# A two-block transformer kernel on one core: the end of the last down-projection and the final norm

## What is computed

```python
T, D, D_FF = 256, 2048, 8192
u = rms_norm_2(h, norm_mlp[l]) @ w_up[l]              # [T, 8192]
h = h + jnp.square(jax.nn.relu(u)) @ w_down[l]        # [T, 2048]
return rms_norm_2(h, norm_final)                      # h * rsqrt(mean(h*h) + 1e-5) * norm_final
```

## Time and profile before

| what | value |
|---|---|
| median of 3 runs | 2543.62 us (2541.82 to 2546.07) |
| span of the profiled execution, first to last instruction | 2541.9 us |
| the profiled execution's own time | the page gives none beside the span |
| PE busy | 2398.7 us (94%) |
| DVE busy | 1389.0 us (55%) |
| ACT busy | 1095.0 us (43%) |
| POOL busy | 48.4 us (2%) |
| chain that ended last: PE banks L2349 | 56% of the span |
| HBM read, written | 491.77 MB, 3.67 MB |

### The profile page before, as it was taken

One profiled execution on the slowest core, in us unless ns is written; L12 is line 12 of the kernel. 1 busy time (PEld: TensorE's weight loads), 2 busy tenths in 40 slices (PEclk: granted clock), 3 DMA queues, 4 the chain that ended last, 5 costly groups with the idle time before them and its releaser, 6 DMA issues.

```text
span 2541.9 us, 29777 instructions
## 1 busy us (share of the span) xinstructions
PE 2398.7 (94%) x12196; PEld 1917.1 (75%) x12196; DVE 1389.0 (55%) x1295; ACT 1095.0 (43%) x1099; POOL 48.4 (2%) x77
## 2 busy tenths in 40 slices
PE   5899999999999999999999679999999999999996
PEld 0487778887577788877887567788888888888885
DVE  0344335556846786666456774655555445545443
ACT  0455545333344444545354533456544434334332
POOL 0100000001000000000000000000000000000000
PEclk6899999999999999999999889999999999999998
DMA  9965455558976696555555001654555555565562
GB/s 391 385 197 156 142 166 168 178 184 319 421 252 201 230 370 198 207 166 172 182 183 166 11 18 31 240 175 161 170 182 183 190 192 190 189 193 188 183 198 99
DMA packets 223184, 497.31 MB, mean 196 GB/s; under 512 B 20824, under 2 KB 22888, under 8 KB 213840
## 3 DMA queue, kind: packets, MB, share of 16 engines
q1 hardware_dynamic: 216528, 458.91, 53.9%
q0 software_dynamic: 6528, 36.56, 3.8%
HBM read 491.77 MB, written 3.67 MB: 195 GB/s over the span
## 4 chain that ended last, share of the span: by engine, by line
PE 63%; DVE 6%; ACT 2%; DMA 2%; issue 1%; DVEq 0%; POOL 0%; ACTq 0%
PE banks L2349 56%; PE banks L2419 2%; DMA raw_eight<-in_w_ada 1%; DVE weights_lo L1397 1%; ACT weights_hi L723 1%; PE banks L2612 1%; PE banks L2731 0%; ACT projected L1099 0%; PE banks L2571 0%; PE banks L2805 0%; DVE residual L1756 0%; DVE residual L1761 0%; PE banks L2708 0%; DVE inverse_products L2137 0%; PE banks L2609 0%
## 5 line engine op out<-in xcount | busy, mean ns | idle before, releaser
L1397 DVE TENSOR_TENSOR weights_lo<-weights_raw,weights_hi 128x2048 fp32r<-128x2048 f32 (+1 forms) x356 | 813.4, 2285 | 879.7 <-ACT weights_hi L723 878.0
L723 ACT ACTIVATE weights_hi<-weights_raw 128x2048 fp32r<-128x2048 f32 (+1 forms) x356 | 680.1, 1911 | 1019.3 <-PE banks L2349 986.3
L2349 PE MATMUL banks<-weights_hi,acts_hi 128*128 128x512 f32 (+1 forms) x2240 | 883.3, 394 | 15.0 <-DVE weights_lo L1397 13.9
L2349 PE MATMUL banks<-weights_lo,acts_hi 128*128 128x512 f32 (+1 forms) x2240 | 872.6, 390 | 0.0
L2349 PE MATMUL banks<-weights_hi,acts_lo 128*128 128x512 f32 (+1 forms) x2240 | 872.5, 389 | 0.0
L2349 PEld LDWEIGHTS banks<-weights_hi,acts_hi 128*128 128x128 f32 x2240 | 422.2, 188 | 116.0 <-issue 31.6
L2349 PEld LDWEIGHTS banks<-weights_hi,acts_lo 128*128 128x128 f32 x2240 | 422.0, 188 | 87.6
L2349 PEld LDWEIGHTS banks<-weights_lo,acts_hi 128*128 128x128 f32 x2240 | 422.4, 189 | 85.0 <-issue 1.2
L2349 PE MATMUL banks<-weights_hi,hidden_hi 128*128 128x512 f32 x320 | 125.3, 392 | 0.5 <-DVE weights_lo L1397 0.5
L2349 PE MATMUL banks<-weights_hi,hidden_lo 128*128 128x512 f32 x320 | 124.6, 389 | 0.0
L2349 PE MATMUL banks<-weights_lo,hidden_hi 128*128 128x512 f32 x320 | 124.5, 389 | 0.0
(11 more groups left out here) (507 smaller groups left out, 1917.4 us busy)
## 6 DMA issues: line engine op xcount, KB each, us to landing
weights_raw<-in_w_in_e SPq DMA_DIRECT2D x80, 1024.0 KB, 5.3
raw_eight<-in_w_ada SPq DMA_DIRECT2D x72, 1024.0 KB, 16.2
weights_raw<-in_w_up SPq DMA_DIRECT2D x64, 1024.0 KB, 5.2
weights_raw<-in_w_down SPq DMA_DIRECT2D x64, 1024.0 KB, 5.1
weights_raw<-in_w_in SPq DMA_DIRECT2D x44, 1024.0 KB, 5.0
weights_raw<-in_w_in_o SPq DMA_DIRECT2D x32, 1024.0 KB, 5.6
weights_raw<-in_w_out_e SPq DMA_DIRECT2D x16, 1024.0 KB, 5.7
gate_chunks<-in_w_ada POOLq DMA_DIRECT2D x16, 1024.0 KB, 6.6
```

The source lines that it names most:

```text
L723: eng.activation(WHI[:, c % 2, :, 0:n], RAW[:, sl, :, 0:n], ACT.Copy).then_inc(hi_ready, 1)
L1397: eng.tensor_tensor(WLO[:, c % 2, :, 0:n], RAW[:, c % 4, :, 0:n], WHI[:, c % 2, :, 0:n].bitcast(F32), ALU.subtract).then_inc(lo_ready, 1)
L2349: ins = eng.matmul(BANKS[:, par * 2 + h, 0:s.n], x[:, t, h * P:(h + 1) * P], w[:, c % 2, k, 0:s.n], start=(kc == 0 and k == 0 and m == 0), ...
```

## The change

- **Order of the last chunk.** In the sixteenth chunk of `down3` PE does the 12 matmuls of half 0 first and signals `upper_full`, then the 12 of half 1 (`chunk_by_half`). For that `down3` is written out instead of looped (`loop=False`) on PE, ACT and SP.
- **Sums and gain per block.** After each block of `down3` DVE adds both halves and signals each (`final_rows`), then multiplies the block by its 512 gain columns into a new tile `out_rows` (`final_gain`, two instructions of 512 columns). In the last block it does this half by half.
- **Squares per block.** ACT squares each block and half as an instruction of 512 columns; those of blocks 0, 1 and 2 stand behind the `hi` of chunks 7, 11 and 15. DVE adds the four partial sums of a half with a small reduction.
- **Scaling.** The reciprocal root scales `out_rows`: ACT the first two blocks, DVE the last two, half by half.
- **Gain load.** It moves to a free place in SBUF and is issued by POOL when `down3` starts.
- **Stores.** SP, not POOL, issues four stores of half a megabyte (half h, two blocks each), in the order first/last of half 0, first/last of half 1.
- Two semaphores are merged into others (the rank weights of stage `lora` and the positions), with the same waits.

The diff, cut to its core:

```diff
     def __init__(self, name, view, nblk, n=NB, kc=4, loop=True, rows_only=False, dest=None, kt0=None, func=None,
                  x=None, acts=None, plain=False, scale=None, summed=False, own_ring=False, rot=0, paired=False, ahead=0,
-                 late=None, gated=None, direct=False):
+                 late=None, gated=None, direct=False, by_half=False):
...
-    NFB = place("final_gain_bcast", 159.5, [P, 4, NB])
+    NFB = place("final_gain_bcast", 175.5, [P, 4, NB])
+    OUTN = place("out_rows", 143.5, [P, 4, 2, NB])
+    SQF = place("final_scratch", 183.5, [P, NB])
...
+    FF = 4
+
     def up(q):
         return Stage(f"up{q}", wv(a["w_up"][0], 0, D, q * D, NB), 4, func=ACT.Relu, acts="x4T", scale=6, ahead=0 if q else 2,
                      dest=lambda b, h: UPN[:, bass.ds(b, 1), h, :])
 
     def down(q):
-        return Stage(f"down{q}", wv(a["w_down"][0], q * D, D, 0, NB), 4, x=HIDDEN[q % 2], acts=f"h{q}T", summed=True)
-
-    FF = 4
+        return Stage(f"down{q}", wv(a["w_down"][0], q * D, D, 0, NB), 4, x=HIDDEN[q % 2], acts=f"h{q}T", summed=True,
+                     loop=q < FF - 1, by_half=q == FF - 1)
+
...
+    FIRST_RANK_IN = 16 * (2 * KT // 8 + 1)
+    UPPER_FULL = {s.name: n + 1 for n, s in enumerate(s for s in stages if s.by_half)}
...
             if s.name == "lora":
-                eng.dma_start(RAW[:, sl, :, 0:288], src[0]).then_inc(S(f"first_rank_landed{sl}"), 16)
+                eng.dma_start(RAW[:, sl, :, 0:288], src[0]).then_inc(cond_landed[sl], 16)
                 eng.dma_start(RAW[:, sl, :, 288:368], src[1]).then_inc(landed[sl], 16)
...
+        if not stop:
+            for h in range(2):
+                rows = out[0, h * P:(h + 1) * P, :].rearrange("p (b n) -> p b n", n=NB)
+                for name, b in (("out_first", 0), ("out_last", 2)):
+                    eng.wait_ge(S(name), h + 1)
+                    eng.dma_start(rows[:, b:b + 2, :], OUTN[:, b:b + 2, h, :]).then_inc(S("stored"), 16)
+            eng.wait_ge(S("stored"), 64)
...
         natural(MEMN, a["mem"][0], "mem_in")
-        eng.wait_ge(S("h_summed"), 1)
+        eng.wait_ge(chunk_used, st["down3"].g0 + 2)
         bcast(NFB, a["norm_final_2"], "final_gain_in")
-        eng.wait_ge(S("out_ready"), 1)
-        store()
...
-        mlp_streams(lambda s, after: stream(s, None, after, not s.summed), hidden_out, 3, 
+        def final_squares(b, *halves):
+            def step():
+                for h in halves:
+                    eng.wait_ge(S("final_rows"), 2 * b + h + 1)
+                    ch.add(eng.activation(SQF[:, :], XN[:, b, h, :], ACT.Square,
+                                          accum_out=STAT[:, 96 + 4 * h + b:97 + 4 * h + b]))
+                    ch.done("final_squares")
+            return step
+
+        final_after = {7: final_squares(0, 0, 1), 11: final_squares(1, 0, 1), 15: final_squares(2, 0, 1)}
+        mlp_streams(lambda s, after: stream(s, None, after | final_after if s.by_half else after, not s.summed), hidden_out, 3,
                     first={0: x4_hi(2, 3), 2: x4_hi(4, 5), 3: lambda: (x4_hi(6, 7)(), rms_squares(XN, 6, Y))})
-        eng.wait_ge(S("h_summed"), 1)
-        rms_squares(XN, 6, UPN)
+        for h in range(2):
+            final_squares(3, h)()
+            root(RSTD[:, 6 + h:7 + h])
+            rms_squares.n += 1
+            eng.wait_ge(S("rstd_ready"), rms_squares.n)
+            ch.add(eng.activation(OUTN[:, 0:2, h, :], OUTN[:, 0:2, h, :], ACT.Copy, scale=RSTD[:, 6 + h:7 + h]))
+            ch.done("out_first")
...
+        def half_full(s, h):
+            if h == 0:
+                eng.wait_ge(S("upper_full"), UPPER_FULL[s.name])
+            else:
+                eng.wait_ge(chunk_used, s.g0 + s.kc * s.nblk + 2)
...
-                if s.summed or s.direct and b == s.nblk - 1:
+                if s.by_half and b == s.nblk - 1:
+                    eng.wait_ge(block_out, 4 + 2 * (s.b0 + b))
+                elif s.summed or s.direct and b == s.nblk - 1:
                     eng.wait_ge(block_out, 4 + 2 * (s.b0 + b))
                     eng.wait_ge(chunk_used, s.g0 + s.kc * (b + 1) + 2)
...
-        mlp_streams(lambda s, after: stream(s, sum_block(s) if s.summed else square, after, s.name != "down3"),
+        def final_gain(b, h):
+            return eng.tensor_tensor(OUTN[:, b, h, :], XN[:, b, h, :], NFB[:, b, :], ALU.mult)
+
+        def final_sum(s, b, h):
+            eng.tensor_tensor(XN[:, b, h, :], XN[:, b, h, :], BANKS[:, ((s.b0 + b) % 2) * 2 + h, :], ALU.add)\
+               .then_inc(block_out, 1)
+            eng.wait_ge(block_out, 4 + 2 * (s.b0 + b) + h + 1)
+            eng.sem_inc(S("final_rows"), 1)
+
+        def final_block(s):
+            def each(b):
+                if b < 3:
+                    for h in range(2):
+                        final_sum(s, b, h)
+                    eng.wait_ge(S("final_gain_in"), 16)
+                    for h in range(2):
+                        ch.add(final_gain(b, h))
+                    return
+                ch.wait()
+                for h in range(2):
+                    half_full(s, h)
+                    final_sum(s, b, h)
+                    ch.link(final_gain(b, h))
+                    if h == 1:
+                        final_scale(0)
+                    final_mean(h)
+                final_scale(1)
+
+            def final_mean(h):
+                eng.wait_ge(S("final_squares"), 7 + h)
+                v = RSTD[:, 6 + h:7 + h]
+                ch.link(eng.tensor_reduce(v, STAT[:, 96 + 4 * h:100 + 4 * h], AX.X, ALU.add))
+                ch.add(eng.tensor_scalar(v, v, 1.0 / D, EPS, ALU.mult, ALU.add))
+                ch.done("square_in")
+
+            def final_scale(h):
+                v = RSTD[:, 6 + h:7 + h]
+                roots[0] += 1
+                eng.wait_ge(S("root_out"), roots[0])
+                ch.add(eng.reciprocal(v, v))
+                ch.done("rstd_ready")
+                ch.add(eng.tensor_scalar(OUTN[:, 2:4, h, :], OUTN[:, 2:4, h, :], v, None, ALU.mult))
+                ch.done("out_last")
+
+            return each
+
+        def mlp_block(s):
+            return final_block(s) if s.by_half else sum_block(s) if s.summed else square
+
+        mlp_streams(lambda s, after: stream(s, mlp_block(s), after, s.name != "down3"),
                     hidden_in, 3,
                     first={2: x4_lo(4, 5), 3: lambda: (x4_lo(6, 7)(), inverse_rms(6))})
-        eng.wait_ge(block_out, 4 + 2 * (st["down3"].b0 + 4))
-        ch.done("h_summed")
-        inverse_rms(6)
-        eng.wait_ge(S("final_gain_in"), 16)
-        for h in range(2):
-            ch.add(eng.scalar_tensor_tensor(out=XN[:, :, h, :], in0=XN[:, :, h, :], scalar=RSTD[:, 6 + h:7 + h],
-                                            in1=NFB[:, :, :], op0=ALU.mult, op1=ALU.mult))
-        ch.done("out_ready")
...
+        def chunk_by_half(s, par, kc, c, g, kt, nk):
+
+            eng.wait_ge(lo_ready, g + 1)
+            xh, xl = s.x or (XTH, XTL)
+            for h in range(2):
+                for k in range(4):
+                    for m, (x, w) in enumerate(((xh, WHI), (xh, WLO), (xl, WHI))):
+                        ins = eng.matmul(BANKS[:, par * 2 + h, 0:s.n], x[:, kt + k, h * P:(h + 1) * P],
+                                         w[:, c % 2, k, 0:s.n], start=(kc == 0 and k == 0 and m == 0),
+                                         stop=(kc == nk - 1 and k == 3 and m == 2))
+                ins.then_inc(*((S("upper_full"), 1) if h == 0 else (chunk_used, 1)))
+
         def chunk(s, B, par, kc, c, g, kt, nk):
...
-                chunk(s, None, (s.b0 + b) % 2, kc, g, g, kt, s.kc)
+                if s.by_half and c == s.nblk * s.kc - 1:
+                    chunk_by_half(s, (s.b0 + b) % 2, kc, g, g, kt, s.kc)
+                else:
+                    chunk(s, None, (s.b0 + b) % 2, kc, g, g, kt, s.kc)
```

More of the change, by code:

```diff
@@ L132, in __init__ @@
         self.direct = direct
+        self.by_half = by_half
         self.rot = rot
@@ L679, in _ @@
         eng.wait_ge(S("gated_z"), 4)
-        eng.dma_start(ROPE[:, 7, 0, 0:2].bitcast(I32), a["positions"]).then_inc(S("positions_in"), 16)
+        eng.dma_start(ROPE[:, 7, 0, 0:2].bitcast(I32), a["positions"]).then_inc(S("second_consts_in"), 16)
         bcast(LNG, a["ln_g"][1], "ln_in")
@@ L720, in hi @@
             if s.name == "lora":
-                eng.wait_ge(S(f"first_rank_landed{sl}"), 16)
+                eng.wait_ge(cond_landed[sl], FIRST_RANK_IN)
             eng.wait_ge(chunk_used, g0 + 4 * i + c + 1)
@@ L1879, in angles @@
         def angles():
-            eng.wait_ge(S("positions_in"), 16)
-            eng.wait_ge(S("second_consts_in"), 16)
+            eng.wait_ge(S("second_consts_in"), 32)
             ch.link(eng.tensor_copy(ROPE[:, 6, 0, 0:2], ROPE[:, 7, 0, 0:2].bitcast(I32)))
```

## The result

The changed kernel takes 2529.21 us (median of 6 executions, 2527.19 to 2531.52) against 2545.1 us for the kernel before in the same series (6 executions, 2541.82 to 2547.58). The ratio is 0.9938 with a 95% interval of 0.9927 to 0.9949: 15.8 us faster, by the interval 13 to 18.6. The forecast was -8.4 us. The sign was right, the size was not. The profiled execution took 2528.68 us, its span is 2526.9 us.

A forecast was written before the change was run, and what follows sets the result against it. PE's unbroken matmuls bound the kernel, so only the 24.6 us tail could shrink: 5.1 us to the last stores' issue and 3.3 us in the stores, -8.4 from the median 2543.62, giving 2535.2 us, range 2532.0 to 2539.0.

The forecast's parts named there:

- the third of the three pieces of the tail: From the last store's landing to the span's end, 2536.3 to 2541.9: 5.6 us, kept unchanged by the forecast.
- The allowance of 1 us either way: Margin on the 5.6 us program end, because how it ends with SP waiting was not shown.
- The last rival: Program's end grows or the tail has unseen waits, some 4 us: 2539, within 0.2%; chance 5%.
- PE had nothing to lose: Up to the last matmul: PE busy 87.10 of 87.10 us in `down3`, no matmul removed, so priced at nothing.
- the forecast said 0.4: DVE at block ends: 1.56 us of added gain products in 1.95 us idle, leaving 0.4.
- The rival that the block ends stop PE: DVE's added work delays `lo` past PE's need, from 3.15 us per block end; 2549 us or more, chance 2%.
- To the issue of the last pair: Tail from the last matmul to half 1's first store: 6.5 us forecast, against 11.6 before.
- From issue to last landing: Half 1's two half-megabyte stores on SP's queue: 2.7 plus 1.3 us, 4.0 in all.
- go one by one: Rival on the four final stores: each pays its own landing before the next moves; -4.8, 2538.8 us, chance 9%.
- the rival's 2: Rival that half order does nothing: half 0's sum waits for the last matmul, about 2 us back, 2537.2; chance 7%.

## Why the prediction was right in sign and wrong in size

*The step that failed* is the third of the three pieces of the tail: "2536.3 to 2541.9, 5.6 us: the program's end. The change does not touch what stands there, except that SP and not POOL waits for the stores". The exception was the whole of it. 5.1 of the 5.6 us were POOL's closing DRAIN, which ran there only because POOL's wait held it back. With the wait on SP the piece is 0.4 us. The forecast wrote that no row split the 5.6; one did, on the program's last line. The allowance of 1 us either way was worked out from nothing. The last rival, that the program's end grows, had the right place and the wrong sign. With the DRAIN in the sum, -8.4 - 5.1 = -13.5, beside -13.9 in the tail.

*What held.* PE had nothing to lose and lost nothing. Its row for the last stage, as the earlier trace rows:

```profile
2429.00:2516.20 87.20, 87.20 (x385) 71.91 (x383) 44.99 (x33) 33.67 (x30) 0.55 (x1) 1.00 0.47 157
```

Two rows were taken for others here, and neither changes the forecast. The stretch 2344 to 2425 of the earlier trace rows is not about `up3` but in `down2` (its matmuls read `hidden_hi`), of which two blocks are written out and two looped. The stretch in `up3`, all written out, says the same:

```profile
2256.00:2341.00 85.00, 85.00 (x388) 70.63 (x387) 43.07 (x27) 35.11 (x27) 0.00 (x0) 1.00 0.58 186
```

And the sum at 2439.98 in the earlier trace rows is that of the last block of `down2`, which stands behind the third `lo` of `down3`. The first of `down3` itself follows four chunks later, with the same idle time behind it:

```profile
2461.74 1.28 DVE L2262 TENSOR_TENSOR residual<-residual,banks 128x512 f32<-128x512 f32 x2
2464.97 2.29 DVE L1397 TENSOR_TENSOR weights_lo<-weights_raw,weights_hi 128x2048 fp32r<-128x2048 f32 x1 [1.96 <-ACT weights_hi L723]
```

DVE's and ACT's work at the block ends fitted where it was put (DVE, then ACT, as the earlier trace rows, at the second block of `down3`):

```profile
2482.40 1.52 DVE L2361 TENSOR_TENSOR residual<-residual,banks 128x512 f32<-128x512 f32 x2
2484.07 1.29 DVE L2358 TENSOR_TENSOR out_rows<-residual,final_gain_bcast 128x512 f32<-128x512 f32 x2
2485.64 2.29 DVE L1424 TENSOR_TENSOR weights_lo<-weights_raw,weights_hi 128x2048 fp32r<-128x2048 f32 x1 [0.28 <-ACT weights_hi L735]
```

```profile
2485.51 0.61 ACT L1400 ACTIVATE final_scratch<-residual 128x512 f32<-128x512 f32 x1
...
2486.33 0.63 ACT L1400 ACTIVATE final_scratch<-residual 128x512 f32<-128x512 f32 x1
...
2489.13 1.92 ACT L735 ACTIVATE weights_hi<-weights_raw 128x2048 fp32r<-128x2048 f32 x1 [2.08 <-PE banks L2436]
```

Of DVE's 1.95 us of idle time 0.28 is left here and at the third block; the forecast said 0.4. At the first block nothing is left (the `lo` starts at 2463.87, as the gain product ends), and PE was busy all the same. The rival that the block ends stop PE had nothing in it.

*The sizes.* To the issue of the last pair, 6.1 against 6.5: the scaling on ACT took 1.15 (1.14 forecast), the square with its read 0.73 (0.82, the two overlap by 0.1), the hop to SP's queue 0.07, not POOL's 0.34. DVE's scaling took 0.75 (0.93). From issue to last landing 4.1 against 4.0.

*The rivals.* The stores did not go one by one: 2.8 to 3.7 us each, overlapping. Half order does what it says, worth 2.25 us against the rival's 2.

*Where the 13.9 us of the tail come from*, from the experiments, if their parts add up: SP waits and issues 5.7 (of it the DRAIN 5.1; the rest is the hop to the issuing queue, a shorter landing and a gain load that landed 0.3 sooner in that execution); the gain load alone 0.0; half order 2.25; two stores into four 0.3; the remaining 5.7 is 13.9 less the others. No run undid that last part by itself, but differences between runs split it in two halves of about 2.9. With SP's stores on the kernel before, the last pair is issued 11.2 us behind the last matmul; on the changed kernel without half order 8.4: that is the norm by block (squares and gain product ahead of the last matmul, the scaling shared by two engines). From that issue to the last landing it was 7.3 us with all the output still to go, and 4.4 when only the second of two megabyte stores was left: that is half 0's output leaving ahead of half 1's.

## What to carry to other kernels

Read the closing line of every engine in the trace before calling the end of a program fixed: if one engine's closing instruction is long, let that engine reach it early, with no transfer of its own still under way, and give the last wait to another. A tail behind the last matmul is a chain like any other, and the place of each short instruction in a queue counts: one reciprocal ahead of a sum instead of behind a product was worth 1.35 us. When a gain is below what the times resolve, read the profile from a fixed point near the change (here the last matmul), where two executions agreed to 0.02 us while their starts differed by microseconds.

## What the runs showed of the hardware that was not expected

POOL's closing DRAIN takes 4.9 to 5.3 us when it starts after everything has landed: 5.13, 4.97, 5.30, 5.11 and 4.89 in five kernels, whether POOL's last own DMA lay 0.2 us or 900 us back, and also with a fill just ahead of it. Started while a DMA of POOL's own is under way, it ends 2.5 to 2.6 us after that has landed (nine profiles, of seven kernels). What it does in that time the traces don't show, and no run took it away. The same instruction takes 7 to 17 ns on ACT and DVE, and on SP where SP has waited for its stores; where SP closes right behind an issue of its own it took 123 to 369 ns (three runs). On PE it takes 4.0 to 4.3 us, beside the last matmuls.

The gain load took 7.4 us to land beside the weight loads, against 4.9 alone at the end of the kernel before. The four weight loads about it took 5.9 (median; the one issued next after it 7.6) against 5.1. The ring of four slots covered both: PE was busy for 87.20 of 87.20 us.
